# Gated delta rule with heads 0, 2 and 1, 3 on the two partition halves, and a chunk's state products for two heads next to each other

## The chip, the cores and the metric

The kernel runs on one core of one Trainium2 chip. The metric is the device time of one execution in microseconds; three executions of the kernel before are known. Engines are named as in the profile: PE (TensorE), DVE (VectorE), ACT (ScalarE), POOL (GpSimd) and SP (SyncE).

## The reference

The model has a first block of two layers (differential attention and a long convolution) and a second of two hybrid layers (gated delta rule, latent attention, a linear recurrence). 512 tokens, width 1024. The change touches only the gated delta rule of the hybrid layers: 4 heads, key and value width 128, chunks of 64 tokens:

```python
def step(state, inp):
    q_n, k_n, u_n, w_n, g_n, a_n = inp
    v_new = u_n - jnp.einsum('bhck,bhkv->bhcv', w_n, state)
    o = jnp.einsum('bhck,bhkv->bhcv', q_n * jnp.exp(g_n)[..., None], state) \
        + jnp.einsum('bhij,bhjv->bhiv', a_n, v_new)
    g_last = g_n[..., -1]
    state = state * jnp.exp(g_last)[..., None, None] + jnp.einsum(
        'bhck,bhcv->bhkv', k_n * jnp.exp(g_last[..., None] - g_n)[..., None], v_new)
    return state, o
```

Before the steps, u and w are made for all chunks at once from a unit lower triangular matrix of 64x64 for each chunk and head, which holds products of keys with decays.

## The kernel before

Activations lie with channels on the partitions and 512 tokens along the free axis. Weights come in pieces through two buffers: SP loads `wraw`, ACT rounds it to `w_hi` (L1221), POOL makes the rest `w_lo` (L2491), and PE multiplies the parts (L609, L618, L623 and for smaller tiles L886, L889, L893 or L922, L924, L926).

`psum_plan` is one list of jobs. A job's place in it gives its PSUM bank, number modulo 8; PE takes the jobs in that order (`take`), and waits at each until the job eight places earlier was emptied. Each engine's code is written out in its own order; nothing is scheduled by a tool.

For the delta rule, a layer (`l` is 0 or 1) goes so:

- DVE sums the gates' logarithms (`decays`), PE spreads them as rows (`gR`, `gB`; L900), and DVE takes the differences of decays for every pair of tokens in a chunk, in `dtm` (L2217 for partitions 0 to 63, L2219 for 64 to 127, for each head). L2224 clips them and ACT takes exponentials (L1607). The second use of the rows, `ltm`, is L2235 and L2237.
- PE makes products of keys with keys and queries (L1014), DVE and PE invert the triangular matrices by doubling (`X`, `XT`; L1041, L1053, L1059), and PE turns keys and values to rows of tokens (L1021), where they are scaled (L2274 for values).
- PE makes `w` (L1072) and `u` (L1079).
- The scan runs over eight chunks (`ck`).

In `dtm`, `vb`, `kg`, `uB` and the other tiles with tokens on the partitions, 128 tokens are a block `tt` and the chunk's parity says which half of the partitions it has: even chunks have partitions 0 to 63, odd ones 64 to 127, for all four heads. Heads lie along the free axis. A chunk of the scan on PE is this:

```python
for h in range(H):
    ins = mm(ps[part, h * P:(h + 1) * P], wT[:, tt, h, part], st[:, ck % 2, h, :],
...
tile("qn", ck)
...
    mm(out[:, h * CH:(h + 1) * CH], st[:, ck % 2, h, :], qg[:, h, ck * CH:(ck + 1) * CH],
...
    ins = mm(ps[:, h * P:(h + 1) * P], kg[part, tt, h, :], vnew[part, tt % 2, h, :],
...
    ins = mm(out[:, h * CH:(h + 1) * CH], vnew[part, tt % 2, h, :], dtm[part, tt, h, :],
```

They are L1090 (job `vn`, w times state), L1096 (job `oc`, state times queries), L1102 (job `su`, the update) and L1106 (adds to `oc`). Between them stand a tile of query weights (`qn`) and at the chunk's end a tile of `kn` (chunks 0 to 3) or `vv` (4 to 7). DVE makes the new values (L2350) and, in four linked steps, the next state (L2357); ACT empties `oc` (L1660). The next `vn` waits for the fourth step.

## Time and profile before

| what | us |
|---|---|
| three executions, median | 2157.35 |
| lowest and highest | 2153.92, 2158.64 |
| the profiled execution, as a whole | 2160.61 |
| its span | 2157.5 |
| PE busy | 2045.2 |
| DVE busy | 1260.0 |
| ACT busy | 907.2 |
| POOL busy | 646.8 |

The span is the time from the first to the last record of the core. The mean granted clock of PE is 0.97 of full speed. Busy times are unions of the intervals in which an engine has an instruction; a float32 product is two MATMUL instructions, and their durations overlap, so the time between two starts, and not the duration, tells what one costs.

### The profile page before, as it was taken

Reading aid. Unit: us, or ns where it says so; the run is one execution under the profiler, and the core shown is the slowest. Engines: PE = TensorE matmul, PEld = TensorE weight load, DVE = VectorE, ACT = ScalarE, POOL = GpSimd, SP = SyncE. Lnnn points to the kernel's source line nnn. Section 1 sums busy time; section 2 is a strip of 40 time slices with the busy share of each in tenths; the row PEclk is TensorE's granted clock in tenths of the full one; section 3 lists DMA queues with packets and bytes.
Section 4 is the critical chain, followed back from the end, with each engine's and each line's share of the span. In section 5 each row is a group of like instructions: output and inputs, shape, how many; then the busy total and the mean of one; then the engine's idle time right before and its main releaser. Section 6 shows DMA issues by size and latency. Waiting matters only on the chain. (4 is left out here: it accounts for less than half of the span.)

```text
span 2157.5 us, 28176 instructions
## 1 busy us (share of the span) xinstructions
PE 2045.2 (95%) x10992; PEld 1546.7 (72%) x10992; DVE 1260.0 (58%) x1994; ACT 907.2 (42%) x1450; POOL 646.8 (30%) x308
## 2 busy tenths in 40 slices
PE   8999999999999999999999898999999988989997
PEld 6667874757668775667786777777877767867776
DVE  4688945547779854456658843535144877264332
ACT  4432255333432345333456444545234734254531
POOL 2323430223414431124443212223433431122252
PEclk9999999998999999999999999999999999989998
DMA  6223321142223231132322001112232210111232
GB/s 223 83 98 108 113 79 49 62 143 98 96 85 117 73 108 53 56 108 83 117 79 69 19 26 52 49 50 103 98 117 78 88 38 15 35 59 41 64 113 86
DMA packets 47858, 174.26 MB, mean 81 GB/s; under 512 B 5646, under 2 KB 6286, under 8 KB 46320
## 3 DMA queue, kind: packets, MB, share of 16 engines
q1 hardware_dynamic: 47600, 172.34, 23.5%
q8 instruction: 88, 1.44, 0.3%
q14 instruction: 42, 0.34, 0.1%
q10 hardware_dynamic: 128, 0.13, 0.0%
HBM read 157.77 MB, written 14.68 MB: 80 GB/s over the span
## 5 line engine op out<-in xcount | busy, mean ns | idle before, releaser
L2491 POOL TENSOR_TENSOR w_lo<-wraw,w_hi 128x1024 fp32r<-128x1024 f32 (+2 forms) x248 | 589.5, 2378 | 1358.1 <-ACT w_hi L1221 1358.1
L1221 ACT ACTIVATE w_hi<-wraw 128x1024 fp32r<-128x1024 f32 (+2 forms) x248 | 253.0, 1020 | 702.1 <-PE bank L623 413.7
L609 PE MATMUL bank<-h_hi,w_hi 128*128 128x512 f32 x1568 | 409.0, 403 | 1.1 <-ACT h_hi L1248 1.1
L618 PE MATMUL bank<-h_lo,w_hi 128*128 128x512 f32 x1568 | 388.7, 390 | 0.2
L623 PE MATMUL bank<-h_hi,w_lo 128*128 128x512 f32 x1536 | 379.5, 389 | 0.0
L609 PEld LDWEIGHTS bank<-h_hi,w_hi 128*128 128x128 f32 x1568 | 293.8, 191 | 92.7 <-issue 32.6
L618 PEld LDWEIGHTS bank<-h_lo,w_hi 128*128 128x128 f32 x1568 | 294.2, 188 | 64.0 <-DVE h_lo L1778 1.7
L623 PEld LDWEIGHTS bank<-h_hi,w_lo 128*128 128x128 f32 x1536 | 288.3, 188 | 59.9
L726 PE MATMUL bank<-arena,wdir 128*128 128x512 f32 x256 | 114.7, 599 | 1.1 <-DMA wdir<-in_w_direct 1.1
L1975 DVE CUSTOM_DVE_ANT_0 arena<-bank,arena 128x512 f32<-128x512 f32 x64 | 44.2, 691 | 89.7 <-PE bank L809 88.4
L726 PEld LDWEIGHTS bank<-arena,wdir 128*128 128x128 f32 x256 | 47.2, 190 | 66.3 <-issue 66.1
L2397 DVE TENSOR_TENSOR bank<-bank,con 128x128 f32<-128x128 f32 x64 | 19.2, 300 | 128.7 <-PE bank L1137 127.5
L2127 DVE SCALAR_TENSOR_TENSOR arena<-bank,colB,arena 128x511 f32<-128x511 f32 (+2 forms) x72 | 53.9, 749 | 61.1 <-ACT arena L1508 59.0
L2446 DVE TENSOR_TENSOR arena<-arena,bank 128x512 f32<-128x512 f32 x16 | 11.0, 687 | 127.4 <-PE bank L623 126.1
L1248 ACT ACTIVATE h_hi<-arena 128x512 fp32r<-128x512 f32 x64 | 39.4, 627 | 66.1 <-DVE arena L2022 37.3
L1697 ACT ACTIVATE arena<-bank,small 128x128 f32<-128x128 f32 (+1 forms) x64 | 33.7, 526 | 74.5 <-DVE small L2400 66.3
L1131 PE MATMUL bank<-arena 128*128 128x128 f32 (+3 forms) x128 | 51.6, 488 | 14.1 <-ACT arena L1501 13.0
L1773 DVE RECIPROCAL rs<-rs 128x512 f32<-128x512 f32 x10 | 33.5, 3353 | 50.0 <-ACT rs L1267 49.9
L1413 ACT ACTIVATE arena<-arena,small 128x512 f32<-128x512 f32 x64 | 46.3, 723 | 30.6 <-DVE small L1979 27.2
L2357 DVE SCALAR_TENSOR_TENSOR arena<-arena,bank 128x128 f32<-128x128 f32 x56 | 19.5, 348 | 51.5 <-PE bank L1102 50.0
L1495 ACT ACTIVATE arena<-bank 128x512 f32<-128x512 f32 x66 | 38.5, 584 | 25.5 <-PE bank L893 25.4
L1144 PE MATMUL bank<-con,arena 128*128 128x128 f32 x160 | 30.5, 293 | 14.8 <-DVE arena L2408 14.8
(403 smaller groups left out, 3267.0 us busy)
## 6 DMA issues: line engine op xcount, KB each, us to landing
wraw<-in_w_split SPq DMA_DIRECT2D x220, 512.0 KB, 3.2
wdir<-in_w_direct SPq DMA_DIRECT2D x16, 512.0 KB, 3.4
x_park<-arena SPq DMA_DIRECT2D x3, 2048.0 KB, 6.3
arena<-x_park SPq DMA_DIRECT2D x3, 2048.0 KB, 8.0
wraw<-in_w_split SPq DMA_DIRECT2D x12, 384.0 KB, 2.9
hg_park<-arena SPq DMA_DIRECT2D x2, 2048.0 KB, 8.7
arena<-hg_park SPq DMA_DIRECT2D x2, 2048.0 KB, 7.8
wraw<-in_w_split SPq DMA_DIRECT2D x16, 256.0 KB, 2.6
```

Of the source, the lines that this page charges most:

```text
L609: mm(ps[0:wd, 0:S], hi[:, k, :].bitcast(F32R), h_hi[:, k, :].bitcast(F32R), start=k == 0 and not begun, stop=False)
L618: ins = mm(ps[0:wd, 0:S], hi[:, k, :].bitcast(F32R), h_lo[:, k, :].bitcast(F32R), start=False, stop=bool(parts) and k == KT - 1)
L623: ins = mm(ps[0:wd, 0:S], lo[:, k, :].bitcast(F32R), h_hi[:, k, :].bitcast(F32R), start=False, stop=k == KT - 1)
L726: ins = mm(ps[:, 0:S], w[:, j % per, k, :], src[:, k, :], start=k == 0, stop=k == kt - 1)
L1131: mm(ps[:, 0:n], qn[:, h, i * P:(i + 1) * P], kn[:, h, 0:n], start=True, stop=False)
L1221: a(w_hi[:, n % 2, 0:f].bitcast(F32R), wraw[:, n % 2, 0:f], ACT.Copy).then_inc(hi_done, 1)
L1248: a(h_hi[:, k, :].bitcast(F32R), src[:, k, :], ACT.Copy).then_inc(up("h_hi", PARTS[ph], k), 1)
L1413: a(LG[:, i % 2, cc, :], LG[:, i % 2, cc, :], ACT.Exp, bias=small[:, 20 + 2 * (i % 2) + cc:21 + 2 * (i % 2) + cc], accum_out=small[:, 24 + ...
L1495: a(dst, bank(*job)[:, 0:S], ACT.Copy).then_inc(release(*job), 1)
L1975: v.tensor_tensor_reduce(LG[:, i % 2, cc, :], bank("s", l, h, i, cc)[:, 0:S], biasT[:, h, b0:b0 + S], 1.0, -3.0e38, ALU.add, ALU.max, smal ...
L2127: ins = v.scalar_tensor_tensor(gqkv(j)[:, lag:S], ps[:, 0:S - lag], cb("gw", 12 * tap + j), gqkv(j)[:, lag:S], ALU.mult, ALU.add)
L2491: nc.gpsimd.tensor_tensor(w_lo[:, n % 2, 0:f].bitcast(F32R), wraw[:, n % 2, 0:f], w_hi[:, n % 2, 0:f], ALU.subtract).then_inc(lo_done, 1)
```

## The change

Tokens of a chunk now lie on the partitions by head parity: heads 0 and 2 on partitions 0 to 63, heads 1 and 3 on 64 to 127, and both chunks of a block along the free axis. A free index of four is 2c + g, with c the chunk's parity and g the half of the head's number. Keys and values are written once in an order (`kpair`, `vpair`) in which a 128-column piece is 64 tokens of two heads, so that the same transposes give the new layout. The columns of gates, made with all tokens on partitions, are copied to it (`gpair`): four small copies by ACT for the decays, and later four by DVE for all.

In the scan the loops over heads run as (g, p), so that two neighbours stand on two halves; `su` and `oc` take two banks each, one for each p. A chunk thereby has seven jobs and not five, and `su` and `oc` have a semaphore step for each p. `vnew` has four buffers. The differences in `dtm` and the products in `ltm` take one DVE operation for each head.

```diff
@@ -155,7 +155,8 @@
             jobs += [(g, l, n, tt) for tt in range(NT) for g in (("dXT", "dX") if n < len(LEVELS) - 1 else ("dXT",))]
...
         for ck in range(NC_):
-            jobs += [("vn", l, ck), ("qn", l, ck), ("oc", l, ck)] + ([("su", l, ck)] if ck < NC_ - 1 else [])
+            jobs += [("vn", l, ck), ("qn", l, ck)] + [("oc", l, ck, p) for p in range(2)]
+            jobs += [("su", l, ck, p) for p in range(2)] if ck < NC_ - 1 else []
...
@@ -328,7 +329,7 @@
...
-                     ("Pm", 2048), ("Mt", 2048), ("spare", 1536), ("gN", 64), ("egl", H * NC_)])
+                     ("Pm", 2048), ("Mt", 2048), ("spare", 1536), ("gN", 64), ("egl", H * NC_), ("gP", 64)])
...
@@ -341,9 +342,9 @@
...
-        wT, uB = view(rb, "Pm", 4, H, P), view(rb, "Mt", 4, H, P)
+        wT, uB = view(rb, "Pm", 4, 2, H, CH), view(rb, "Mt", 4, H, P)
...
-        vnew = arena[:, rb["X"] + 1024:rb["X"] + 2048].rearrange("p (b h c) -> p b h c", b=2, h=H)
+        vnew = arena[:, rb["X"] + 1024:rb["X"] + 2048].rearrange("p (b g c) -> p b g c", b=4, g=2)
...
@@ -393,6 +394,10 @@
...
+        gP = view(rb, "gP", 64)
+        gpair = gP.rearrange("p (t r n) -> p t r n", t=NT, r=4)
+        kpair, vpair = ([arena[:, at:at + 1024].rearrange("p (k h i) -> p k h i", k=NC_, h=2) for at in ats]
+                        for ats in ((rb["XT"] + 1024, rb["X"] + 1024), (rb["oa"], rb["oa"] + 1024)))
...
@@ -412,9 +417,22 @@
...
-        def own_tokens(a, c):
-
-            return a.rearrange("p (t c i) -> p t c i", t=NT, c=2)[:, :, c, :]
+        def by_chunk(a):
+
+            return a.rearrange("p (t c i) -> p t c i", t=NT, c=2)
+
+        def in_chunks(a):
+
+            return a.rearrange("p (k i) -> p k i", k=NC_)
+
+        def pair_of(a, h):
+
+            return a[h // 2][:, :, h % 2, :]
+
+        def blocks(tt):
+
+            return [(n, p, 2 * (n % 2) + p, slice(tt * P + CH * (n // 2), tt * P + CH * (n // 2) + CH))
+                    for n in range(H) for p in range(2)]
...
@@ -1005,20 +1023,18 @@
...
-                for kind, other in (("kk", kB), ("qk", qB)):
+                for kind in ("kk", "qk"):
                     for tt in range(NT):
...
-                        for h in range(H):
-                            for c in range(2):
-                                own = slice(tt * P + CH * c, tt * P + CH * c + CH)
-                                ins = mm(ps[halves[c], h * CH:(h + 1) * CH], kB[:, h, own], other[:, h, own],
-                                         start=True, stop=True)
+                        for n, p, h, own in blocks(tt):
+                            ins = mm(ps[halves[p], n * CH:(n + 1) * CH], kpair[n % 2][:, 2 * tt + n // 2, p, :],
+                                     kpair[n % 2][:, 2 * tt + n // 2, p, :] if kind == "kk" else qB[:, h, own], start=True, stop=True)
...
                     for tt in range(NT):
...
-                        for h in range(H):
-                            ins = nc.tensor.transpose(ps[:, h * P:(h + 1) * P], src[:, h, tt * P:(tt + 1) * P], ident)
+                        for n in range(H):
+                            ins = nc.tensor.transpose(ps[:, n * P:(n + 1) * P], src[n % 2][:, 2 * tt + n // 2, :, :].rearrange("p h i -> p (h i)"), ident)
...
@@ -1043,7 +1059,7 @@
...
-                        natural(TURN_AT[n], {"kN": kB, "vN": vB}[TURN_AT[n]])
+                        natural(TURN_AT[n], {"kN": kpair, "vN": vpair}[TURN_AT[n]])
                     for tt in range(NT):
...
@@ -1083,29 +1099,32 @@
...
                 for ck in range(NC_):
...
-                    part = slice(off, off + CH)
-                    pe.wait_ge(*(read("su", l, ck - 1) if ck else after("state0", l)))
+                    c = ck % 2
+                    pairs = [(g, p, part) for g in range(2) for p, part in enumerate(halves)]
+                    pe.wait_ge(*(read("su", l, ck - 1, 1) if ck else after("state0", l)))
...
-                    for h in range(H):
-                        ins = mm(ps[part, h * P:(h + 1) * P], wT[:, tt, h, part], st[:, ck % 2, h, :],
+                    for g, p, part in pairs:
+                        ins = mm(ps[part, g * P:(g + 1) * P], wT[:, tt, p, 2 * c + g, :], st[:, ck % 2, 2 * g + p, :],
...
                     tile("qn", ck)
-                    out = take("oc", l, ck)
-                    for h in range(H):
-                        mm(out[:, h * CH:(h + 1) * CH], st[:, ck % 2, h, :], qg[:, h, ck * CH:(ck + 1) * CH],
-                           start=h == 0, stop=False)
+                    out = [take("oc", l, ck, p) for p in range(2)]
+                    for g, p, part in pairs:
+                        mm(out[p][:, g * CH:(g + 1) * CH], st[:, ck % 2, 2 * g + p, :], qg[:, 2 * g + p, ck * CH:(ck + 1) * CH],
+                           start=g == 0, stop=False)
                     pe.wait_ge(*read("vn", l, ck))
                     if ck < NC_ - 1:
-                        ps = take("su", l, ck)
-                        for h in range(H):
-                            ins = mm(ps[:, h * P:(h + 1) * P], kg[part, tt, h, :], vnew[part, tt % 2, h, :],
+                        new = [take("su", l, ck, p) for p in range(2)]
+                        for g, p, part in pairs:
+                            ins = mm(new[p][:, g * P:(g + 1) * P], kg[part, tt, 2 * c + g, :], vnew[part, ck % 4, g, :],
...
-                        ins.then_inc(filled("su", l, ck), 1)
-                    for h in range(H):
-                        ins = mm(out[:, h * CH:(h + 1) * CH], vnew[part, tt % 2, h, :], dtm[part, tt, h, :],
-                                 start=False, stop=h == H - 1)
-                    ins.then_inc(filled("oc", l, ck), 1)
+                            if g == 1:
+                                ins.then_inc(filled("su", l, ck, p), 1)
+                    for g, p, part in pairs:
+                        ins = mm(out[p][:, g * CH:(g + 1) * CH], vnew[part, ck % 4, g, :], dtm[part, tt, 2 * c + g, :],
+                                 start=False, stop=g == 1)
+                        if g == 1:
+                            ins.then_inc(filled("oc", l, ck, p), 1)
...
@@ -1575,7 +1594,7 @@
...
-                    a(gqkv(j), gqkv(j), ACT.Silu).then_inc(up("gc_sb", l, j), 1)
+                    a(gqkv(j) if j < 8 else pair_of(vpair, j - 8), gqkv(j) if j < 8 else in_chunks(gqkv(j)), ACT.Silu).then_inc(up("gc_sb", l, j), 1)
...
@@ -1586,6 +1605,11 @@
...
                 silu_z(2)
+                act.wait_ge(*after("decays", l))
+                for p in range(2):
+                    for c in range(2):
+                        ins = a(gpair[halves[p], :, 1, 2 * c:2 * c + 2], gcol4[halves[c], :, 1, p:H:2], ACT.Copy)
+                ins.then_inc(up("gc_pair", l), 1)
                 silu_z(3)
...
@@ -1647,8 +1671,8 @@
...
-                        a(wT[:, 2 * pr:2 * pr + 2, :, part].rearrange("p t h i -> p (t h) i"),
-                          bank("w", l, pr, c)[:, :].rearrange("p (n i) -> p n i", i=CH), ACT.Copy).then_inc(release("w", l, pr, c), 1)
+                        a(wT[:, 2 * pr:2 * pr + 2, c, :, :],
+                          bank("w", l, pr, c)[:, :].rearrange("p (t n i) -> p t n i", t=2, i=CH), ACT.Copy).then_inc(release("w", l, pr, c), 1)
...
@@ -1656,10 +1680,11 @@
...
                 for ck in range(NC_):
...
-                    act.wait_ge(*full("oc", l, ck))
-                    a(oa[:, :, ck * CH:(ck + 1) * CH],
-                               bank("oc", l, ck)[:, 0:H * CH].rearrange("p (h i) -> p h i", h=H), ACT.Copy).then_inc(release("oc", l, ck), 1)
-                    act.wait_ge(*read("oc", l, ck))
+                    for p in range(2):
+                        act.wait_ge(*full("oc", l, ck, p))
+                        a(oa[:, p:H:2, ck * CH:(ck + 1) * CH],
+                          bank("oc", l, ck, p)[:, 0:P].rearrange("p (g i) -> p g i", g=2), ACT.Copy).then_inc(release("oc", l, ck, p), 1)
+                        act.wait_ge(*read("oc", l, ck, p))
...
@@ -2214,28 +2239,32 @@
...
-                    link(v.tensor_tensor(dtm[halves[0], :, h, :], own_tokens(bank("gB", l, h, 1)[halves[0], 0:S], 0),
-                                         gcol4[halves[0], :, 1, h:h + 1].broadcast_to([CH, NT, CH]), ALU.subtract))
-                    v.tensor_tensor(dtm[halves[1], :, h, :], own_tokens(bank("gB", l, h, 1)[halves[1], 0:S], 1),
-                                    gcol4[halves[1], :, 1, h:h + 1].broadcast_to([CH, NT, CH]),
+                    if h == 0:
+                        dve.wait_ge(*after("gc_pair", l))
+                    part, g = halves[h % 2], h // 2
+                    v.tensor_tensor(dtm[part, :, g:H:2, :], by_chunk(bank("gB", l, h, 1)[part, 0:S]),
+                                    gpair[part, :, 1, g:H:2].unsqueeze(3).broadcast_to([CH, NT, 2, CH]),
...
                 for tt in range(NT):
...
-                    v.scalar_tensor_tensor(gqkv(j), gqkv(j), P ** -0.5 if j < 4 else 1.0,
-                                           bank("lb", l, j)[:, 0:S], ALU.mult, ALU.mult).then_inc(release("lb", l, j), 1)
+                    if j < 4:
+                        v.scalar_tensor_tensor(qB[:, j, :], qB[:, j, :], P ** -0.5, bank("lb", l, j)[:, 0:S],
+                                               ALU.mult, ALU.mult).then_inc(release("lb", l, j), 1)
+                    else:
+                        v.scalar_tensor_tensor(pair_of(kpair, j - 4), in_chunks(gqkv(j)), 1.0, in_chunks(bank("lb", l, j)[:, 0:S]),
+                                               ALU.mult, ALU.mult).then_inc(release("lb", l, j), 1)
...
                 for tt in range(NT):
...
-                    link(v.tensor_tensor(ltm[halves[0], :, h, :], dtm[halves[0], :, h, :],
-                                         own_tokens(bank("gB", l, h, 0)[halves[0], 0:S], 0), ALU.mult))
-                    v.tensor_tensor(ltm[halves[1], :, h, :], dtm[halves[1], :, h, :],
-                                    own_tokens(bank("gB", l, h, 0)[halves[1], 0:S], 1), ALU.mult).then_inc(release("gB", l, h, 0), 1)
+                    part, g = halves[h % 2], h // 2
+                    v.tensor_tensor(ltm[part, :, g:H:2, :], dtm[part, :, g:H:2, :],
+                                    by_chunk(bank("gB", l, h, 0)[part, 0:S]), ALU.mult).then_inc(release("gB", l, h, 0), 1)
...
@@ -2250,7 +2279,7 @@
...
-                    return gN[:, n:n + H].unsqueeze(2).broadcast_to([P, H, P])
+                    return gP[:, n:n + H].unsqueeze(2).broadcast_to([P, H, P])
...
@@ -2289,6 +2318,10 @@
...
                 second_level(3)
...
+                for p in range(2):
+                    for c in range(2):
+                        ins = v.tensor_copy(gpair[halves[p], :, :, 2 * c:2 * c + 2], gcol4[halves[c], :, :, p:H:2])
+                link(ins)
...
@@ -2343,23 +2376,24 @@
...
                 for ck in range(NC_):
...
-                    part = slice(off, off + CH)
+                    c = ck % 2
                     dve.wait_ge(*full("vn", l, ck))
...
-                        dve.wait_ge(*full("oc", l, ck - 4))
-                    v.tensor_tensor(vnew[part, tt % 2, :, :], uB[part, tt, :, :], bank("vn", l, ck)[part, :].rearrange("p (h i) -> p h i", h=H), ALU.subtract).then_inc(release("vn", l, ck), 1)
+                        dve.wait_ge(*full("oc", l, ck - 4, 1))
+                    v.tensor_tensor(vnew[:, ck % 4, :, :], uB[:, tt, 2 * c:2 * c + 2, :], bank("vn", l, ck)[:, 0:2 * P].rearrange("p (g i) -> p g i", g=2), ALU.subtract).then_inc(release("vn", l, ck), 1)
...
                     if ck < NC_ - 1:
...
-                            dve.wait_ge(*full("oc", l, ck - 1))
-                        dve.wait_ge(*full("su", l, ck))
+                            dve.wait_ge(*full("oc", l, ck - 1, 1))
...
+                            if h < 2:
+                                dve.wait_ge(*full("su", l, ck, h))
...
-                                                            bank("su", l, ck)[:, h * P:(h + 1) * P], ALU.mult, ALU.add)
-                            if h == H - 1:
-                                ins.then_inc(release("su", l, ck), 1)
-                                dve.wait_ge(*read("su", l, ck))
+                                                            bank("su", l, ck, h % 2)[:, (h // 2) * P:(h // 2 + 1) * P], ALU.mult, ALU.add)
+                            if h >= 2:
+                                ins.then_inc(release("su", l, ck, h - 2), 1)
+                                dve.wait_ge(*read("su", l, ck, h - 2))
...

```

On PE, second chunk of the scan of the first layer, with the banks. The names: bank and what is read; `arena` is the one large buffer; a row is one line of code with its repetitions. Before:

```order
L1090 MATMUL bank3<-arena 64x128 x4
L886 MATMUL bank4<-rows,w_hi 128x512 x3
L889 MATMUL bank4<-rows,w_lo 128x512 x3
L893 MATMUL bank4<-kr_parts,w_hi 128x512 x3
L1096 MATMUL bank5<-arena 128x64 x4
L1102 MATMUL bank6<-arena 128x128 x4
L1106 MATMUL bank5<-arena 128x64 x4
L886 MATMUL bank7<-ckv_hi,w_hi 128x512 x2
```

The update's products and the output's after it, in the same chunk, in the kernel after:

```order
L1119 MATMUL bank1<-arena 128x128
L1119 MATMUL bank2<-arena 128x128
L1119 MATMUL bank1<-arena 128x128
L1119 MATMUL bank2<-arena 128x128
L1124 MATMUL bank7<-arena 128x64
L1124 MATMUL bank0<-arena 128x64
L1124 MATMUL bank7<-arena 128x64
L1124 MATMUL bank0<-arena 128x64
L904 MATMUL bank3<-ckv_hi,w_hi 128x512 x2
```

The number of products is the same; the four of a group go to two banks in turn, and the order of the groups and tiles has not moved.

On DVE, where the differences of decays are made (`rows` is written by the operation before; the next is L2224, after it L2250). Before:

```order
L2214 TENSOR_TENSOR arena<-arena 128x4x4
L2217 TENSOR_TENSOR arena<-bank,arena 64x4x64
L2219 TENSOR_TENSOR arena<-bank,arena 64x4x64
L2217 TENSOR_TENSOR arena<-bank,arena 64x4x64
L2219 TENSOR_TENSOR arena<-bank,arena 64x4x64
L2217 TENSOR_TENSOR arena<-bank,arena 64x4x64
L2219 TENSOR_TENSOR arena<-bank,arena 64x4x64
L2217 TENSOR_TENSOR arena<-bank,arena 64x4x64
L2219 TENSOR_TENSOR arena<-bank,arena 64x4x64
L2224 TENSOR_SCALAR arena<-arena 128x256 x4
```

The same place in the kernel after:

```order
L2221 SCALAR_TENSOR_TENSOR rows<-rs,con,rows 128x512
L2239 TENSOR_TENSOR arena<-arena 128x4x4
L2245 TENSOR_TENSOR arena<-bank,arena 64x8x64 x4
L2250 TENSOR_SCALAR arena<-arena 128x256 x4
L2254 SCALAR_TENSOR_TENSOR arena<-arena,bank 128x512 x4
```

Eight operations have become four of twice the free size. On ACT, ahead of the rows' rounding (L1591 before, L1615 after), the kernel after has:

```order
L1592 ACTIVATE tmp<-bank 128x512
L1611 ACTIVATE arena<-arena 64x4x2 x4
L1592 ACTIVATE tmp<-bank 128x512
L1615 ACTIVATE rows<-bank 128x512
L1617 ACT_TABLE_LOAD
```

Four small copies have come between the last two of the recurrence's gates, which stood one behind the other (L1573, x2) before.

## Rows read from the trace of the kernel before

**Rows 1.** The page: busy time, share of the span and instructions of each engine.
```profile
PE 2045.2 (95%) x10992; PEld 1546.7 (72%) x10992; DVE 1260.0 (58%) x1994; ACT 907.2 (42%) x1450; POOL 646.8 (30%) x308
```

**Rows 2.** Stretches: length, busy us (count) PE, PEld, DVE, ACT, POOL; clock, DMA, GB/s.
```profile
1269.98:1328.67 58.69, 58.69 (x381) 50.60 (x381) 15.23 (x36) 15.90 (x29) 10.29 (x7) 1.00 0.10 32
1831.84:1890.52 58.68, 58.68 (x380) 50.59 (x381) 15.22 (x36) 15.90 (x29) 10.28 (x7) 1.00 0.10 32
1261.50:1263.43 1.93, 1.93 (x33) 1.86 (x33) 1.19 (x3) 1.72 (x3) 1.07 (x1) 1.00 0.00 0
1161.23:1162.99 1.76, 1.76 (x9) 1.46 (x9) 1.57 (x1) 1.62 (x3) 0.00 (x0) 1.00 0.04 9
1174.03:1177.26 3.23, 3.23 (x9) 2.55 (x9) 3.13 (x7) 0.00 (x0) 1.20 (x1) 0.50 0.30 87
```

**Rows 3.** Timeline of PE, one chunk: start, time, engine, line, operation, shapes, count.
```profile
1277.63 1.09 PE L1090 MATMUL bank<-arena 128*64 128x128 f32 x8
1278.64 0.97 PE L886 MATMUL bank<-rows,w_hi 128*128 128x512 f32 x3
...
1281.77 1.16 PE L1102 MATMUL bank<-arena 64*128 64x128 f32 x8
1282.76 1.00 PE L1106 MATMUL bank<-arena 64*128 64x64 f32 x8
1283.69 0.74 PE L886 MATMUL bank<-ckv_hi,w_hi 128*128 128x512 f32 x2
...
1285.28 0.32 PE L1090 MATMUL bank<-arena 128*64 128x128 f32 x1
```

**Rows 4.** Timeline of PE in windows of 0.02 us at group ends.
```profile
1270.57 0.49 PE L1090 MATMUL bank<-arena 128*64 128x128 f32 x3
...
1270.79 0.27 PE L1090 MATMUL bank<-arena 128*64 128x128 f32 x1
...
1282.43 0.50 PE L1102 MATMUL bank<-arena 64*128 64x128 f32 x3
...
1282.65 0.27 PE L1102 MATMUL bank<-arena 64*128 64x128 f32 x1
...
1263.00 0.50 PE L1072 MATMUL bank<-arena 64*128 64x64 f32 x6
...
1263.22 0.28 PE L1072 MATMUL bank<-arena 64*128 64x64 f32 x2
```

**Rows 5.** Timeline of the first scan: PE's update products, DVE's values and state.
```profile
1274.11 1.16 PE L1102 MATMUL bank<-arena 64*128 64x128 f32 x8
...
1275.75 1.50 DVE L2357 SCALAR_TENSOR_TENSOR arena<-arena,bank 128x128 f32<-128x128 f32 x4 [3.87 <-PE bank L1102]
...
1278.82 0.69 DVE L2350 TENSOR_TENSOR arena<-arena,bank 64x512 f32<-64x512 f32 x1 [1.58 <-PE bank L1090]
...
1283.06 1.50 DVE L2357 SCALAR_TENSOR_TENSOR arena<-arena,bank 128x128 f32<-128x128 f32 x4 [3.55 <-PE bank L1102]
```

**Rows 6.** Timeline from the last gates to PE's wait, first layer.
```profile
1157.65 1.20 ACT L1573 ACTIVATE tmp<-bank 128x512 f32<-128x512 f32 x2 [4.34 <-DVE arena L2201]
...
1162.74 0.22 ACT L1597 ACTIVATE arena<-arena 128x16 f32<-128x16 f32 x1
...
1166.46 0.41 DVE L2217 TENSOR_TENSOR arena<-bank,arena 64x256 f32<-64x256 f32 x1
...
1169.64 0.43 DVE L2219 TENSOR_TENSOR arena<-bank,arena 64x256 f32<-64x256 f32 x1
...
1170.11 0.90 DVE L2224 TENSOR_SCALAR arena<-arena 128x256 f32<-128x256 f32 x4
...
1170.13 0.56 PE L900 MATMUL bank<-rows,sel 4*128 4x512 f32 x1 [0.42 <-DVE arena L2219]
...
1173.31 0.79 PE L900 MATMUL bank<-rows,sel 4*128 4x512 f32 x1 [2.62 <-ACT arena L1495]
```

**Rows 7.** Timeline of DVE where values are scaled, first layer.
```profile
1209.39 2.48 DVE L2274 TENSOR_TENSOR arena<-bank,arena 128x512 f32<-128x512 f32 x4 [1.48 <-PE bank L1021]
```

4 lines of the change are left out of this document (2 added, 2 removed).

## The prediction

> **What bounds the kernel now.** The page first: TensorE's matmuls fill 2045.2 of 2157.5 us, 95% of the span [rows 1]. So the kernel is a TensorE kernel as a whole, but that says nothing yet of the stretch that is changed. For that I read the two state scans by stage. The scan of the first layer runs from 1269.98 to 1328.67, that of the second from 1831.84 to 1890.52; both take 58.7 us, TensorE is busy in all of it, at a granted clock of 1.00, while VectorE works 15.23 us and ScalarE 15.90 us of it [rows 2]. TensorE is the bound there with nothing idle. Then I read one chunk in order of time [rows 3]: from 1277.63 to 1285.28, 7.65 us, and the eight chunks of both layers repeat it (the last has no state update). In it stand the products of w with the state (L1090, from 1277.63 to 1278.64, 1.01 us), a query tile of latent attention (L886 and its mates), the products of the state with the queries (L1096), the state update's products (L1102, 1281.77 to 1282.76, 0.99 us), those of the masked attention with the new values (L1106, 1282.76 to 1283.69, 0.93 us) and a key or value tile (L886, 1283.69 to 1285.28, 1.59 us). Each of the four groups has 8 instructions in the trace, two for each of four float32 products.
>
> **What a product costs alone and side by side.** The steps between single instructions at the end of a group show it [rows 4]. In L1090 the third from last starts at 1270.57 and the last at 1270.79: 0.11 us each. In L1102 the like rows are 0.22 us apart for two steps as well, 0.11 each. In L1072 (which makes w, and whose products alternate between the two halves of the rows and two banks) the row that begins at 1263.00 holds six instructions and the last two start at 1263.22: two steps of 0.11 us, but two instructions at each. That is a pair that costs what one costs. The whole group of L1072, 32 instructions (the view counts one neighbour more), lies within 1.93 us [rows 2], 0.06 each, where L1090 takes 0.126 [rows 3].
>
> **The change, part by part.** *The scan.* Before, the four heads of a chunk use the same half of the array, since a chunk's tokens are on one half of the partitions. After, heads 0 and 1, and then 2 and 3, stand on different halves and follow each other in the program: 4 steps of 0.11 us in place of 8, so a group gets 4 x 0.11 = 0.44 us shorter. What it pays once, at its start and end, stays. Three groups change so: L1090 (column halves), L1102 and L1106 (row halves, into two banks); L1096 uses all rows and columns and stays. A chunk with a state update gains 3 x 0.44 = 1.32 us, the last 2 x 0.44 = 0.88. A layer gains 7 x 1.32 + 0.88 = 10.1 us and both 20.2. The nearest row for L1102 isn't exact: L1072 streams 64 columns, L1102 will stream 128 in each half. The low bound is that nothing of the three groups overlaps (0), the high bound is half of each group, edges too, (1.01 + 0.99 + 0.93) / 2 = 1.47 us a chunk, 8 x 1.47 x 2 = 23.4 less 2 x 0.50 for the missing update, 22.4. I take 20.2, by the steps in the rows.
>
> The Trainium skill, page "TensorEngine Tiling (Array Packing)", section "Tiling Modes", says that different tiles can load weights and multiply in parallel, and its overview gives up to 2x for a dimension of 64 or less. Taken as a full halving it would give the 22.4 us; the rows with their edges give 20.2, and the trace decides.
>
> *What TensorE would wait for next.* The next chunk's first product needs the new state, which VectorE makes from L1102's result. The update starts at 1283.06, 1.29 us after L1102's first instruction, and its four steps take 1.50 us [rows 5]. With L1102 shorter by 0.44 it starts 0.85 us after it and ends at 2.35; a product that waits for VectorE follows it by about 0.06 us (VectorE's L2219 ends at 1170.07, TensorE's row starts at 1170.13 [rows 6]). The second of the four steps waits for another bank as well; I count 0.05 for that: 2.46. TensorE's own work from the same instant is 0.99 - 0.44, 0.93 - 0.44 and 1.59: 2.63 us. So it is still TensorE that comes last, by 0.17 us, where the same count gives 3.51 against 2.85, 0.66 us, before. I cost this at nothing, and the cover is the key or value tile. Without that tile each chunk would wait 1.4 us.
>
> *The other work in the scan.* The new values become one operation on 128 partitions and 256 columns in place of 64 and 512 (0.69 us, L2350 [rows 5]), shorter, and behind it TensorE has a whole query tile: nothing. ScalarE empties two banks in place of one, 16 more small copies at no more than the 0.60 us of a 128x512 one in rows 6, 8 a layer: under 5 us beside 15.90 of 58.7 [rows 2], nothing. A chunk takes seven banks in place of five. Every job waits for the one eight jobs earlier; the youngest of these is the first output bank of the chunk before, and between its filling and its reuse stand 1.59 us of the key tile, the shorter L1090 and a query tile. Behind such a wait the rest of TensorE's queue would stand; none is late. The three jobs of weight preparation keep their order and have about 6.3 us a chunk in place of 7.65.
>
> *Before the scan: decays.* The differences of decays become 4 operations of 64x512 in place of 8 of 64x256. Before, from 1166.46 (L2217) to the start of L2224 at 1170.11 they take 3.65 us [rows 6]. A 64x512 operation with a bank takes 0.69 us [rows 5], with 0.04 between two: 2.92. This is 0.7 us a layer, and it is on the path: L2224, exponentials, ScalarE's L1495, and only then TensorE goes on at 1173.31 after 2.62 us idle [rows 6]. Against it stand four new little copies by ScalarE ahead of the last gate, between the two L1573 at 1157.65, from which the same chain leads on by rows, roots and reciprocal. A small ScalarE operation takes 0.22 us (L1597 [rows 6]); four take between 0 (cover by another wait) and 0.88. I take 0.5, since overlapping neighbours show less than their length. Net gain 0.2 us a layer, 0.4 in both (bounds -0.4 and 1.4).
>
> *Edits with one answer.* The four little copies by VectorE after the chunk masks lie in its 1.48 us of idle before L2274 [rows 7]: if each takes no more than one of the four bigger L2224 (0.90 us together [rows 6]) they need 0.9 and fit. The products of decays and write strengths (L2235, L2237) become half as many, but TensorE then has two whole tiles to do: nothing. Silu and scaling only write in other places; transposes and the 64x64 products keep number and shape; kbe, kg, vb and w keep theirs. Nothing moves on SyncE or GpSimd.
>
> **The sum.** 20.2 + 0.4 = 20.6 us. The profiled span is 2157.5 us; it would be 2136.9. That execution took 2160.6 us as a whole, 3.3 above the median of 2157.35; from the median I get 2157.35 - 20.6 = 2136.8 us.
>
> **The rivals.** *The state chain takes over.* For it: the margin of 0.17 us is the smallest in the sum, and the first update of the first layer began at 1275.75, 1.64 us after its L1102 at 1274.11, 0.35 later than the next ones [rows 5]. If all 14 updates come 0.35 later, 14 x (0.35 - 0.17) = 2.5 us are lost: 2139.3; with L2357's steps longer by a tenth too, about 2141. Against it: the later updates keep 1.29. The Trainium skill, the same page, section "Performance Considerations", warns of just this, that after a tiling speedup the emptying of PSUM may be the bottleneck; by the rows it is close and doesn't decide.
>
> *Row halves with 128 columns don't overlap.* L1102 then stays at 0.99 us: 14 x 0.44 = 6.2 us less gain, 2143.0. If L1106 doesn't either, 2150.0. For it: no row shows a full 128 columns streamed by both row halves into full-width outputs. Against it: L1072 reaches two at a time with the same weights and the same two banks.
>
> *It doesn't do what it says:* the products stay one behind another, and the time is 2157 or, with the decays, 2156.8. Against it L1072 in rows 4.
>
> *Slower: the clock.* If the engine's clock fell during the packed scan, a product costs double: eight L609 at a granted 0.50 take 3.23 us against 1.76 at 1.00 [rows 2]. Place: the scans, 48.6 us each after the change. All of it at the lower of the two levels, 1.2 in place of 2.4 GHz, costs 97 us: 2234. From 20.6 us of full-speed work at that level on, the change is slower than before. Against it: the packed L1072 stretch was granted 1.00 [rows 2], and the scan stays without idle time; before the fall in rows 6 TensorE had stood for 2.62 us. The Trainium skill, "TensorE: Matmul & The Clock Gate", Part 1, lets the clock follow how busy the array has been; how packed products count there it doesn't say, so this rule can't rule the case out.
>
> **How the numbers follow.** Forecast 0.72 (2136.8, itself from 2133 to 2139: the bounds of the decays, and low-clock stretches that fall on other work; one tile's third at the low level costs 1.5 us [rows 2]). State chain 0.12. Row halves 0.08. Nothing done 0.03. Clock 0.05, of which nearly all is slower. For eight in ten the range takes forecast, state chain and half of the row-half case: 2132.5 to 2143.5. About 0.2% (4.3 us) is what a measurement of this kernel can tell from no change. Faster 0.92, same 0.03, slower 0.05.
>
> **What would show it.** After: both scans near 48.6 us with TensorE busy throughout and chunks 6.3 us apart; two instructions at each step in the three groups; L1096's twin as long as before; VectorE's update ending about 0.2 us before TensorE needs it. Chunks of 6.5 or more with an idle mark before the state product are the state chain; an unchanged 0.99 us group for the update is the second rival; a granted clock of 0.5 in the scan the last. TensorE's idle time before the first stretch of L609 at 1174 should end 0.2 us earlier. I am wrong in size if other stretches, the same in both programs, differ by over 2 us together.

## The result and the profile after

The changed kernel takes 2140.35 us (median of four executions, 2139.4 to 2144.6) against 2157.22 for the kernel before, measured beside it: 0.9914 of the time, 95% interval 0.9892 to 0.9936. That is 16.9 us between the medians, where 2136.8 (20.6 less) was forecast. The two profiled spans, 2157.5 and 2137.4, lie 20.1 apart. The page of the kernel after answers to [rows 1]:

```profile
PE 2025.7 (95%) x10992; PEld 1528.7 (72%) x10992; DVE 1255.0 (59%) x1986; ACT 912.0 (43%) x1474; POOL 650.0 (30%) x308
```

TensorE has the same 10992 matmuls, and is busy 19.5 us less. Lines of the code moved: L1090 is now L1107, L1096 is L1113, L1102 is L1119, L1106 is L1124, L886 is L904, L1072 and L1079 are L1088 and L1095, L900 is L918, L609 is L627, L1495 is L1514, VectorE's L2357 and L2350 are L2391 and L2383. The two scans as stretches (length, busy time and count of PE, PEld, DVE, ACT and POOL, granted clock), to be read beside the first two of [rows 2]:

```profile
1271.67:1320.26 48.59, 48.59 (x380) 40.52 (x381) 13.11 (x36) 17.13 (x36) 9.93 (x7) 1.00 0.12 39
1822.47:1871.15 48.68, 48.63 (x380) 40.51 (x380) 13.11 (x36) 17.12 (x36) 9.94 (x7) 1.00 0.12 39
```

They were 58.69 and 58.68 us: 10.1 and 10.0 less, with TensorE busy in 48.59 and 48.63 us of it, at a clock of 1.00. One chunk of the kernel after in order of time, TensorE first and then VectorE, beside [rows 3] and [rows 5]:

```profile
1277.99 0.66 PE L1107 MATMUL bank<-arena 128*64 128x128 f32 x8
1278.58 0.97 PE L904 MATMUL bank<-rows,w_hi 128*128 128x512 f32 x3
...
1280.76 1.00 PE L1113 MATMUL bank<-arena 128*128 128x64 f32 x8
1281.69 0.72 PE L1119 MATMUL bank<-arena 64*128 64x128 f32 x8
1282.24 0.56 PE L1124 MATMUL bank<-arena 64*128 64x64 f32 x8
1282.73 0.73 PE L904 MATMUL bank<-ckv_hi,w_hi 128*128 128x512 f32 x2
...
1284.32 0.44 PE L1107 MATMUL bank<-arena 128*64 128x128 f32 x4
...
1282.54 1.50 DVE L2391 SCALAR_TENSOR_TENSOR arena<-arena,bank 128x128 f32<-128x128 f32 x4 [3.35 <-PE bank L1119]
```

From 1277.99 to 1284.32 a chunk takes 6.33 us instead of 7.65. From start to start L1107 takes 0.59 (it was 1.01), L1119 0.55 (0.99), L1124 0.49 (0.93), and L1113 still 0.93: 0.42, 0.44 and 0.44 less. How the products stand side by side is seen in two narrow windows in the middle of a group; in the serial groups of [rows 4] such a window holds three instructions, here six:

```profile
1278.15 0.50 PE L1107 MATMUL bank<-arena 128*64 128x128 f32 x6
...
1281.91 0.50 PE L1119 MATMUL bank<-arena 64*128 64x128 f32 x6
```

Put on one line, the places of the two profiled executions are these:

| place | before | after | after less before |
|---|---|---|---|
| first scan begins | 1269.98 | 1271.67 | +1.69 |
| it ends | 1328.67 | 1320.26 | -8.41 |
| second scan begins | 1831.84 | 1822.47 | -9.37 |
| it ends | 1890.52 | 1871.15 | -19.37 |
| span | 2157.5 | 2137.4 | -20.1 |

The scans give 20.1 us by these rows. The three stretches outside of them differ by +1.69, -0.96 and -0.73 us and cancel: that the spans differ by just what the scans give is chance in part. Ahead of the first scan the changed kernel is late. The timeline of that stretch, beside [rows 6] (first ScalarE, then TensorE and VectorE):

```profile
1158.40 0.60 ACT L1592 ACTIVATE tmp<-bank 128x512 f32<-128x512 f32 x1 [4.34 <-DVE arena L2226]
1158.90 0.85 ACT L1611 ACTIVATE arena<-arena 64x8 f32<-64x8 f32 x4
...
1161.96 0.86 PE L918 MATMUL bank<-rows,sel 16*128 16x512 f32 x4 [1.23 <-DVEq L2233]
1162.75 3.00 PE L627 MATMUL bank<-h_hi,w_hi 128*128 128x512 f32 x8
...
1167.98 2.85 DVE L2245 TENSOR_TENSOR arena<-bank,arena 64x512 f32<-64x512 f32 x4
...
1174.07 0.79 PE L918 MATMUL bank<-rows,sel 4*128 4x512 f32 x1 [2.69 <-ACT arena L1514]
```

The four new copies (L1611) take 0.85 us, and TensorE waits 1.23 us ahead of the rows of decays. In the kernel before it is 0.45:

```profile
1160.45 0.86 PE L900 MATMUL bank<-rows,sel 16*128 16x512 f32 x4 [0.45 <-DVEq L2208]
```

So they stand on the path almost whole, 0.78 of 0.85. Right behind them, the granted clock is 0.50 for a while, and eight L627 take 3.00 us where they take 2.12 in the kernel before at the same place:

```profile
1163.75:1166.50 2.75, 2.75 (x8) 2.10 (x7) 2.54 (x1) 2.71 (x7) 0.00 (x0) 0.50 0.00 0
```

That low clock costs nothing in this place, since TensorE has to wait for L1514 all the same: from L918 at 1161.96 to that wait's end at 1174.07 it is 12.11 us, and 12.10 in the run below that has the full clock there.

At the last row of the timeline above the changed kernel is 0.76 us late (1174.07 against 1173.31), but 0.74 of it is older than any changed code: the last group of weights ahead of the gate begins at 1154.96 (L627) against 1154.22 (L609), and TensorE has been 0.74 us behind since 1018 us, in work that is the same in both kernels. From that group to the last row it is 19.11 us and was 19.09: the copies' 0.78 us and what the merged differences save cancel. From there to the scan another 0.93 us comes up, 97.60 us against 96.67, at a mean clock of 0.90 against 0.93.

### The profile page after: what moved, and what is told of

Read it like the earlier page. It is cut to its first block, busy times and chain, and to the rows that moved or that the text cites. A ratio compares the mean times of both kernels' runs of the same rounds, so it can differ in the third digit from the quotient of the medians.

```text
span 2137.4 us, 28240 instructions
## 1 busy us (share of the span) xinstructions
PE 2025.7 (95%) x10992; PEld 1528.7 (72%) x10992; DVE 1255.0 (59%) x1986; ACT 912.0 (43%) x1474; POOL 650.0 (30%) x308
## 4 chain that ended last, share of the span: by engine, by line
PE 71%; DVE 21%; ACT 5%; issue 2%; DMA 1%; DVEq 0%; ACTq 0%
PE bank L627 13%; PE bank L636 12%; PE bank L641 12%; PE bank L744 4%; PE bank L756 2%; PE bank L1170 2%; PE bank L1150 2%; PE bank L672 1%; PE bank L827 1%; PE bank L904 1%; PE bank L841 1%; DVE arena L1964 1%; DVE arena L1968 1%; PE bank L764 1%; DVE arena L1966 1%
## 5 line engine op out<-in xcount | busy, mean ns | idle before, releaser
L627 PE MATMUL bank<-h_hi,w_hi 128*128 128x512 f32 x1568 | 410.2, 404 | 1.1 <-ACT h_hi L1267 1.1
L636 PE MATMUL bank<-h_lo,w_hi 128*128 128x512 f32 x1568 | 391.7, 392 | 0.2
L627 PEld LDWEIGHTS bank<-h_hi,w_hi 128*128 128x128 f32 x1568 | 294.1, 191 | 92.6 <-issue 32.5
L636 PEld LDWEIGHTS bank<-h_lo,w_hi 128*128 128x128 f32 x1568 | 296.9, 189 | 65.0 <-DVE h_lo L1803 1.7
L2391 DVE SCALAR_TENSOR_TENSOR arena<-arena,bank 128x128 f32<-128x128 f32 x56 | 19.5, 348 | 48.6 <-PE bank L1119 47.2
L1514 ACT ACTIVATE arena<-bank 128x512 f32<-128x512 f32 x66 | 38.6, 585 | 21.2 <-PE bank L911 21.1
L2501 POOL TENSOR_TENSOR arena<-arena,con 128x256 f32<-128x256 f32 x32 | 24.4, 785 | 69.3 <-PE bank L1057 69.3
```

Source lines behind the costliest of these rows:

```text
L627: mm(ps[0:wd, 0:S], hi[:, k, :].bitcast(F32R), h_hi[:, k, :].bitcast(F32R), start=k == 0 and not begun, stop=False)
L636: ins = mm(ps[0:wd, 0:S], hi[:, k, :].bitcast(F32R), h_lo[:, k, :].bitcast(F32R), start=False, stop=bool(parts) and k == KT - 1)
```

## The experiments

**The same kernel again.** The gain between medians was 3.7 us short of the forecast, that between spans only 0.5. So the changed kernel was measured once more, with six executions.

> The kernel after, unchanged, timed beside the others on one chip. Theory (side-by-side products save 20.2 us, the stretch before the scan gives some back): the time is 16 to 21 us below the kernel before. In its trace both scans last 48.6 us. Where PE reaches the first scan, 1.7 us later than before in the first execution (1271.67 against 1269.98), a repeat should lie again 0.5 to 2.5 us later; if that was only where the low clock happened to fall, it may lie earlier as well.

Measured: 2142.22 us (2141.62 to 2145.15), 0.9923 of the kernel before (0.9907 to 0.9939). The chunks again stand 6.32 to 6.33 us apart. But TensorE reaches the first scan at 1275.22, 5.2 us later than in the kernel before, where at most 2.5 was expected, and 3.55 later than in the first execution of the same kernel; 3.3 of these arise between 1174.34 and 1275.22, 100.88 us against 97.60, which no difference of program can explain. The span is 2140.4, 3.0 longer. The medians of the same kernel differ by 1.9 us, and those of the kernel before lay between 2157.2 and 2159.7 beside the various kernels. A difference of 2 us between two kernels is therefore not read from whole times here, but from stretches.

**The copies alone.** The kernel before with nothing added but the four copies by ScalarE, at the same place, into a tile that nobody reads:

```diff
+                act.wait_ge(*after("decays", l))
+                for p in range(2):
+                    for c in range(2):
+                        ins = a(gpair[halves[p], :, 1, 2 * c:2 * c + 2], gcol4[halves[c], :, 1, p:H:2], ACT.Copy)
+                ins.then_inc(up("gc_pair", l), 1)
```

> The kernel before with one part of the change alone: ScalarE's four small copies of decays between its last two gates, into columns that nobody reads. Theory A (they delay the chain to the rows of decays by their own 0.88 us): PE's idle before L900 at 1160.45 grows from 0.45 to 1.3 us and everything after it is 0.9 us a layer later, or 2 us and more where the low clock then comes in the L609 stretch behind it; time 1 to 5 us above the kernel before. Theory B (hidden): no change.

Measured: 2159.49 us (2154.62 to 2163.89), 0.9999 of the kernel before (0.9984 to 1.0014), so nothing that the whole time could show; the 1 to 5 us of theory A are not in it. TensorE's wait in the trace of this kernel is there, as theory A says:

```profile
1163.80 0.85 PE L902 MATMUL bank<-rows,sel 16*128 16x512 f32 x4 [1.23 <-DVEq L2215]
1164.58 2.12 PE L611 MATMUL bank<-h_hi,w_hi 128*128 128x512 f32 x8
```

The wait is 1.23 as in the changed kernel, and the eight L611 behind it take 2.12 us: here the clock did not fall. The copies cost 0.78 us a layer at this place; the low clock behind them in the changed kernel is not their doing by itself.

**The copies moved.** The changed kernel with the copies ahead of the third silu of the gate, where ScalarE waits for VectorE anyway:

```diff
-                silu_z(2)
                 act.wait_ge(*after("decays", l))
...
                 ins.then_inc(up("gc_pair", l), 1)
+                silu_z(2)
                 silu_z(3)
```

> The kernel after with ScalarE's four small copies of decays one step earlier, ahead of the third gate, where ScalarE stood idle for 4.34 us (L1573 before, L1592 after). Theory A (the copies are on the path): the row of L918 that began at 1161.96 after 1.23 us of idle begins 0.88 us earlier with an idle of about 0.4, the stretch of L627 behind it stays at full clock as in the kernel before (1.76 us for 8 in place of about 2.8), and the time is 2 to 4 us below that of the kernel after for both layers. Theory B (the copies are hidden anyway and the loss is chance of the clock): the row moves by less than 0.3 us, no difference beyond 1 us in the median.

Measured: 2140.15 us (2135.21 to 2144.56), 0.9911 (0.9891 to 0.9932). TensorE's wait is back where it was, and the eight L627 behind take 2.11 us:

```profile
1160.92 0.86 PE L918 MATMUL bank<-rows,sel 16*128 16x512 f32 x4 [0.46 <-DVEq L2233]
...
1173.02 0.79 PE L918 MATMUL bank<-rows,sel 4*128 4x512 f32 x1 [2.69 <-ACT arena L1514]
```

Theory A stands in the rows. The 2 to 4 us that it promised for the whole time are not shown: the median is 0.2 below the first one of the changed kernel and 2.1 below the one measured beside it, with executions from 2135.21 to 2144.56. From 1160.92 to 1173.02 it is 12.10 us; the kernel before takes 12.86 (1160.45 to 1173.31). The 0.76 between them is what remains of the change here once the copies are out of the way.

**The differences split again.** To see whether this 0.76 is the merging of eight operations to four, the changed kernel got eight back:

```diff
-                    v.tensor_tensor(dtm[part, :, g:H:2, :], by_chunk(bank("gB", l, h, 1)[part, 0:S]),
...
+                    for c in range(2):
+                        ins = v.tensor_tensor(dtm[part, :, 2 * c + g, :], by_chunk(bank("gB", l, h, 1)[part, 0:S])[:, :, c, :],
```

> The changed kernel with the differences of decays as eight operations of 64x256 again and not four of 64x512; layout and everything else as changed. Theory A (the term of the merged differences: four took 2.85 us where eight took 3.65, and they stand on the path to the exponentials for which TensorE waits): from the gate rows to the end of TensorE's wait is 0.7 to 0.8 us longer than the 12.1 to 12.2 us with four, and the scans stay at 48.3. Theory B (fixed cost isn't what the eight paid; the second of TensorE's own rows comes last): not longer by more than 0.2 us.

Measured once (2144.92 us):

```profile
1162.79 0.86 PE L918 MATMUL bank<-rows,sel 16*128 16x512 f32 x4 [1.23 <-DVEq L2233]
...
1168.81 3.61 DVE L2246 TENSOR_TENSOR arena<-bank,arena 64x256 f32<-64x256 f32 x8
...
1175.65 0.79 PE L918 MATMUL bank<-rows,sel 4*128 4x512 f32 x1 [2.52 <-ACT arena L1514]
```

From 1162.79 to 1175.65 it is 12.86 again. The eight take 3.61 us where the four take 2.85, and the 0.76 goes through to TensorE whole; the second layer shows the same, 12.87 against 12.10. Theory A stands.

**A longer state chain.** Whether VectorE's chain really is the next thing behind TensorE in the scan, and how far, is asked with two more linked steps of 0.38 us, which repeat the update of head 0 and change nothing:

```diff
+                            for _ in range(2 if h == 0 else 0):
+                                link(v.scalar_tensor_tensor(st[:, (ck + 1) % 2, h, :], st[:, ck % 2, h, :],
...
```

> The changed kernel with two steps of the state update of head 0 written out twice more, so that the chain of linked steps on VectorE behind the state products is six steps long and not four; nothing else changes. A step takes about 0.38 us, so the new state is ready 0.75 to 0.77 us later. Theory A (the next thing behind TensorE in a chunk is this chain, with the margin that the trace of the changed kernel shows: the chain ends 0.28 us before the next chunk's first product starts, and 0.06 of that is the way from VectorE to TensorE): the margin of 0.22 us is used up and the rest shows, 0.53 to 0.55 a chunk. Chunks take 6.86 us instead of 6.33, a scan 7 x 0.54 = 3.8 us more than its 48.3, 52.1, and TensorE shows idle time ahead of the w products of chunks 1 to 7. Theory B (the chain has room, because TensorE fetches work from behind or the margin is larger than it looks): chunks stay at 6.33 and scans at 48.3. Theory C (the chain already holds TensorE, unseen in the rows): all of the 0.76 shows, chunks of 7.09 and scans of 53.6.

Measured once (2150.71 us). TensorE's rows of two chunks and VectorE's last four steps, which begin 0.77 after the two added ones (at 1281.15):

```profile
1276.63 0.66 PE L1107 MATMUL bank<-arena 128*64 128x128 f32 x8 [0.76 <-ACT arena L1679]
...
1283.47 0.66 PE L1107 MATMUL bank<-arena 128*64 128x128 f32 x8 [0.44 <-DVE arena L2395]
...
1290.35 0.66 PE L1107 MATMUL bank<-arena 128*64 128x128 f32 x8 [0.47 <-DVE arena L2395]
...
1281.92 1.50 DVE L2395 SCALAR_TENSOR_TENSOR arena<-arena,bank 128x128 f32<-128x128 f32 x4
```

The chunks are 6.84 and 6.88 us long, 0.51 and 0.55 more, and TensorE has idle time ahead of the state product, released by VectorE. Of 0.77 us more in the chain 0.53 show, so the margin was 0.24 us. Theory A stands; the cover is nearly used up, and what makes TensorE another 0.3 us shorter in a chunk gives nothing without a shorter chain.

**Two products of one half first.** The prediction laid the overlap to neighbours in the program that stand on different halves. Here both heads of one half come first, in all three groups:

```diff
-                    pairs = [(g, p, part) for g in range(2) for p, part in enumerate(halves)]
+                    pairs = [(g, p, part) for p, part in enumerate(halves) for g in range(2)]
```

> The kernel after with the order of the four products turned in every group of the scan: first both heads of the lower half, then both of the upper. Layout, banks, waits and all else stay. Theory A (what saves is that neighbours stand on different halves): only the step in the middle of a group may overlap, each group is 0.22 to 0.44 us longer, a scan takes 53 to 58.7 us (48.6 with the order of the change), the time 9 to 20 us more than the kernel after. Theory B (the layout alone saves, for instance by shorter outputs or by queues inside the engine that find the free half): scans stay at 48.6 us.

Measured: 2140.95 us (2139.65 to 2145.11), 0.9919 (0.99 to 0.9938). The first scan, from 1272.66 to the work behind it at 1321.99, is 49.33 us against 48.59, and not 58.7 (to the start of its own last instruction, as later expectations count, 49.0 against 48.3). One chunk:

```profile
1272.66 0.66 PE L1107 MATMUL bank<-arena 128*64 128x128 f32 x8 [0.76 <-ACT arena L1679]
...
1276.92 0.66 PE L1124 MATMUL bank<-arena 64*128 64x64 f32 x8
...
1279.08 0.66 PE L1107 MATMUL bank<-arena 128*64 128x128 f32 x8
...
1321.99 0.51 PE L940 MATMUL bank<-w_hi,ckv_hi 128*128 128x256 f32 x2
```

L1107 and L1119 are as short as in the changed kernel (0.59, and 0.55 from 1276.37 to 1276.92), only L1124 takes 0.10 us more (0.59 to its successor at 1277.51), one step of a product. The theory that neighbours must alternate falls; theory B, that the layout alone is enough, holds but for this step. Products of the second half start beside those of the first though four instructions stand between. So how far apart may they be?

**Rows of eight and sixteen.** Outside the scan the same was done with longer rows: four products (8 instructions) of one half first for u and for the products of keys and queries (L1030), eight (16 instructions) for w.

```diff
-                    for n in range(H) for p in range(2)]
+                    for p in range(2) for n in range(H)]
...
-                    for tt in (2 * pr, 2 * pr + 1):
-                        for h in range(H):
-                            for c, part in enumerate(halves):
+                    for c, part in enumerate(halves):
+                        for tt in (2 * pr, 2 * pr + 1):
+                            for h in range(H):
...
-                        for h in range(H):
-                            for c in halves:
+                        for c in halves:
+                            for h in range(H):
```

> The changed kernel with the order of products changed outside of the scan, so that a longer row of neighbours stands on the same half of the array before the other half's turn: products of keys and queries four (8 instructions) and not one, u four, and w eight (16 instructions) before the other eight. The run with two products of one half first kept nearly all of the overlap in the scan (49.0 us against 48.3, and 58.2 with none). Theory A (TensorE finds work of the other half only a few instructions ahead, enough for four): the 32 instructions of w, 1.93 us, take about twice that, up to 3.7, and u and the others likewise, up to 3.7 in place of 1.9; the scans stay at 48.3. Theory B (each half takes its own instructions however far they stand apart, as long as they are queued): w 1.9 to 2.1 us and u 1.9 to 2.1 us, as before. Between the two: w with 16 loses its overlap and u with 8 keeps it.

Measured once: 2159.96 us, 18 to 20 above the two medians of the changed kernel and no better than the kernel before. L1030 in the first layer, and in the second the first w, the last u and TensorE's first row in the scan (between them L1095 at 1830.72 took 2.56, and L1088 at 1833.22 took 3.86):

```profile
1194.70 4.99 PE L1030 MATMUL bank<-arena 128*64 128x64 f32 x128
...
1827.40 3.39 PE L1088 MATMUL bank<-arena 64*128 64x64 f32 x32
...
1837.01 4.70 PE L1095 MATMUL bank<-arena 64*64 64x128 f32 x32
1842.46 1.12 PE L1107 MATMUL bank<-arena 128*64 128x128 f32 x8 [0.75 <-ACT arena L1679]
```

The same in the changed kernel:

```profile
1194.78 3.95 PE L1030 MATMUL bank<-arena 128*64 128x64 f32 x128
...
1813.99 2.00 PE L1088 MATMUL bank<-arena 64*128 64x64 f32 x32
1815.92 1.96 PE L1095 MATMUL bank<-arena 64*64 64x128 f32 x32
...
1822.47 0.66 PE L1107 MATMUL bank<-arena 128*64 128x128 f32 x8 [0.76 <-ACT arena L1679]
```

At a row of sixteen the overlap is nearly lost, at rows of eight a part of it: w as the first answer of the expectation says, u between its answers. The last L1088 and L1095 and the start of the scan ran at a lower clock (L1107 1.12 us long and not 0.66), which no answer had: TensorE had no idle time before it. Two more runs follow it up.

**w alone.** Only the second of the three edits.

> The changed kernel with only the order of w's products changed, all eight products (16 instructions) of one half before those of the other; u and the products of keys and queries stay as changed. In the run with all three reordered, w took 3.39 to 3.86 us at a granted clock of 1.00 in place of 2.00, and in both layers the clock fell to 0.50 in the stretch of w and u and stayed low into the scan, where TensorE had no idle time before it fell. Theory A (the overlap goes with the row of 16): w again takes 3.4 to 3.6 us, at least 1.4 more for each of the four, and u stays at 1.96. Theory C (the fall of the clock follows from a stretch in which one half of the array works alone, whichever products it is): it falls here too, somewhere between the second w and the scan, and one or both scans begin at 0.50. Theory D (it follows from u's row of eight or from the length of the whole stretch without overlap, 15 us): the clock stays at 1.00 there and the loss is the 1.4 to 1.6 us for each w.

Measured once (2149.92 us). Rows of TensorE, and then stretches with the clock (between the two rows stand L1095 at 1266.80, 1.96 us long, and L1088 at 1268.69, 3.39 again):

```profile
1263.48 3.39 PE L1088 MATMUL bank<-arena 64*128 64x64 f32 x32
...
1272.01 3.10 PE L1095 MATMUL bank<-arena 64*64 64x128 f32 x32
...
1268.69:1272.01 3.32, 3.32 (x34) 3.25 (x32) 0.65 (x2) 1.19 (x2) 0.00 (x0) 1.00 0.02 5
1272.80:1275.10 2.30, 2.30 (x22) 1.91 (x18) 0.00 (x0) 0.60 (x1) 0.00 (x0) 0.50 0.00 0
...
1829.06:1832.30 3.24, 3.24 (x31) 3.24 (x32) 0.00 (x0) 1.20 (x2) 0.00 (x0) 0.50 0.00 0
```

Each w costs 1.39 us more, as theory A says. And in both layers the granted clock fell to 0.50 behind the second of them, in u, whose order is unchanged, and the first scan began at it. Theory C stands for these products, D falls.

**u alone.** Only the last edit.

> The changed kernel with only the order of u's products changed, four products (8 instructions) of one half before those of the other. Theory A (the overlap is partly kept in a row of eight, as in the one stretch of the run with all three where the clock was granted in full, 2.56 us in place of 1.96): u takes 2.5 to 2.6 us, w stays at 2.00, and four stretches of u cost 2.4 us together. Theory B (that 2.56 came from its neighbours): u takes 2.0 or 3.5 us. On the clock: theory C as in the run with w alone says that it falls here as well, though the halves work alone for less of the time; theory D says that it doesn't.

Measured once (2145.69 us): all four stretches of L1095 are alike, and the clock stays.

```profile
1264.45 2.00 PE L1088 MATMUL bank<-arena 64*128 64x64 f32 x32
1266.38 2.56 PE L1095 MATMUL bank<-arena 64*64 64x128 f32 x32
...
1264.45:1274.00 9.55, 8.93 (x129) 8.37 (x128) 3.66 (x7) 7.69 (x13) 1.27 (x1) 1.00 0.09 29
```

On the overlap theory A stands. On the clock C said that it falls here too, and it didn't; so what C should say is that the fall came with w's rows of sixteen, in which one half works alone for most of the stretch, and not with u's rows of eight.

**A version that goes further.** The copies moved, and besides the rounding of the decays' rows (ScalarE L1615 in the kernel after, and VectorE's L2221 on them) ahead of the last works on the gate, here ScalarE's part against the run with the copies moved:

```diff
                 ins.then_inc(up("gc_pair", l), 1)
-                silu_z(2)
-                silu_z(3)
                 act.wait_ge(*full("gR", l))
                 a(rows[:, 1, :].bitcast(F32R), bank("gR", l)[:, 0:S], ACT.Copy).then_inc(up("row_hi", l, 0), 1)
+                silu_z(2)
+                silu_z(3)
```

> The changed kernel with ScalarE's four copies of decays moved ahead of the third silu of the gate, as in the run where they alone were moved, and besides the rounding of the decays' rows ahead of it too, and VectorE's remainder of them ahead of its last two products with the gate. Theory A (TensorE's wait ahead of the gates' rows, 0.46 us where only the copies were moved, is the wait for ScalarE's and VectorE's last works on the gate): that wait goes to 0.1 or less and another 0.3 to 0.5 us a layer are won against the copies alone, 1.5 to 2.5 us against the changed kernel unmoved: a median of 2138 to 2140. Theory B (the later sigmoids and products of the gate, which now come after, hold the next jobs for as long): nothing is won beyond the 0.85 us a layer of the copies, 2140 to 2141. Stretches of low clock that fall elsewhere can hide a difference of this size in the whole time; the stretch before the scan shows it in the rows.

Measured: 2138.05 us (2136.86 to 2141.89), 0.9907 of the kernel before (0.9885 to 0.9928). The wait is gone altogether:

```profile
1156.26 2.14 PE L627 MATMUL bank<-h_hi,w_hi 128*128 128x512 f32 x8
...
1161.97 0.51 PE L918 MATMUL bank<-rows,sel 16*128 16x512 f32 x4
```

From the last three groups of weights to the wait for L1514 it is now 1156.26 to 1174.11, 17.85 us, where the run with the copies moved took 18.34 (1154.68 to 1173.02) and the changed kernel 19.11 (1154.96 to 1174.07, some of it at the low clock). Theory A stands for the stretch. The median is the lowest of all kernels, 2.3 to 4.2 us below the two of the changed kernel, but the intervals of the ratios overlap: that this version is faster than the changed kernel is seen in the rows and not yet shown by the whole times.

## Why the prediction was right, and where not

- *The scan, 20.2 us.* Right, and the step that carries the forecast: 10.1 and 10.0 by the rows, 1.32 a chunk. Four steps of 0.11 us in place of eight gave 0.42 to 0.44 a group, and the rest of a group, its start and end, stayed, as was said. The Trainium skill, "TensorEngine Tiling (Array Packing)", "Theoretical Speedup", gives up to 2x; the groups became 1.7 to 1.9 times as fast (1.01 to 0.59, 0.99 to 0.55, 0.93 to 0.49), so the sum by edges was nearer than the full halving of 22.4.
- *The reason for the overlap* was half right. It isn't the alternation of neighbours that does it: with two products of one half first the scan lost 0.1 us a chunk and no more. Only at eight instructions in a row does it begin to go.
- *The state chain.* Right to a few hundredths: the update starts 0.85 us after L1119 and takes 1.50, TensorE's own work from there is 2.63. The margin was put at 0.17 with 0.05 for a second bank; the two added steps measured 0.24. The rival failed because 13 of the 14 updates start 0.81 to 0.85 after their L1119, among them the first of the scan, which came 0.35 late in the kernel before. One did come late as the rival has it, the last of the second scan:

```profile
1864.10 0.71 PE L1119 MATMUL bank<-arena 64*128 64x128 f32 x8
1865.30 1.50 DVE L2391 SCALAR_TENSOR_TENSOR arena<-arena,bank 128x128 f32<-128x128 f32 x4 [3.72 <-PE bank L1119]
```

  It starts 1.20 after its L1119, and this chunk takes 6.45 us (1860.40 to 1866.85): 0.13 lost, about the 0.35 less the margin. The kernel's repetition and the run with the copies moved have it at the same chunk. Why this update is late the runs don't show.
- *Row halves with 128 columns.* They overlap as those with 64 do: L1119 and L1124 each got 0.44 shorter. The rival falls.
- *The differences of decays, 0.7 us a layer.* Right: 0.76, on the path whole.
- *ScalarE's four copies, 0.5 us a layer.* Mis-sized. I took a value between 0 and 0.88 because neighbours overlap in their records; the row of four is 0.85 long, and 0.78 of it reach TensorE, since ScalarE goes on with the last silu only behind them and that leads on to the rows. The net of this section is nothing, (0.76 - 0.78), where I had 0.2 a layer gained.
- *VectorE's four copies* were to fit into its idle time. They do:

```profile
1209.35 0.74 DVE L2323 COPY arena<-arena 64x32 f32<-64x32 f32 x4
1212.27 2.48 DVE L2303 TENSOR_TENSOR arena<-bank,arena 128x512 f32<-128x512 f32 x4 [2.18 <-PE bank L1037]
```

  Behind them VectorE still waits 2.18 us for TensorE before it scales the values.
- *The clock.* It stayed at 1.00 in both packed scans. The rival falls for this kernel, yet a fall of the clock under a busy TensorE exists. It showed where the halves of the array worked one after the other (the runs on w), and there L1107 took 1.12 us in place of 0.66 and L1095 4.70 in place of 2.56.
- *The sum.* By rows it is 20.1 for the scans and nothing for the decays. The spans are 20.1 apart as well, but there luck helped: the other stretches differ by up to 1.69 us and cancel. The idle time that was to end 0.2 us earlier ended 0.02 later, counted from the L627 at 1154.96. The forecast said 2136.8, the median was 2140.35, 3.5 above and inside the range. What is left must lie in stretches that are alike in both programs, as far as the profiled executions tell: the two of the changed kernel itself are 3.0 us apart with equal chunks, more than the 2 us that the prediction set as its sign of a wrong size. It started from the median of before less 20.6; but both kernels' executions scatter by 5 us (2139.4 to 2144.6; 2153.92 to 2158.64). Rows of the same work at either clock show one source of it: eight L636 at 1178.37 in the kernel after take 3.12 us, the same products in the kernel before (L618 at 1177.46) 1.99. Where the low clock falls in each execution is not settled by these runs; only the profiled ones show it.

## What to carry to other kernels

Where a chain of small products uses half of the array, lay the data so that two of them use different halves: count the steps between single instructions in the trace, halve those, and keep the edges. The order in the program may be loose, but keep rows of one half to four instructions. And put the new small copies that such a layout asks for where their engine waits already; at their natural place they ate the whole side gain here. Before making TensorE's part of a loop shorter still, measure the margin of the chain behind it by lengthening the chain.
